# One attention state for the linear-attention layer, a new order of its steps, and identity products on TensorE ahead of the first projection

## What is computed

```python
c_act = jax.nn.silu(c)
for i in range(DEPTH):
    mod = (c_act @ ada_w[i] + ada_b[i])[:, None, :]
    sh1, sc1, g1, sh2, sc2, g2 = jnp.split(mod, 6, axis=-1)
    h = rms_norm(x, norm_mix_g[i]) * (1 + sc1) + sh1
    y = gla_mixer(...) if i % 2 == 0 else moba_mixer(...)
    x = x + g1 * y
    h = rms_norm(x, norm_mlp_g[i]) * (1 + sc2) + sh2
    x = x + g2 * sq_relu_mlp(h, mlp_w1[i], mlp_w2[i])

# gla_mixer, per chunk of 64 tokens, G = cumulated log decay inside the chunk
q_dec = q * exp(G); k_inv = k * exp(-G); k_tail = k * exp(G_last - G)
A = where(causal, q_dec @ k_inv.T, 0)
U = k_tail.T @ v;  S_next = exp(G_last) * S + U
o = A @ v + q_dec @ S
o = rms_norm(o) * silu(r);  y = o @ w_out
```

## Time and profile before

| | |
|---|---|
| median of 3 runs | 641.33 us (641.04 to 641.89) |
| the profiled execution | 641.9 us |
| span in its trace | 640.1 us, so 1.8 us lie around it |
| TensorE busy | 616.4 us of the span |
| TensorE's mean granted clock | 0.991 |
| DMA | 156.4 MB, 244 GB/s over the span; about 385 GB/s from 6 to 36 us |

### The profile page before, as it was taken

One profiled execution on the slowest core, in us unless ns is written; L12 is line 12 of the kernel. 1 busy time (PEld: TensorE's weight loads), 2 busy tenths in 40 slices (PEclk: granted clock), 3 DMA queues, 4 the chain that ended last, 5 costly groups with the idle time before them and its releaser, 6 DMA issues.

```text
span 640.1 us, 9098 instructions
## 1 busy us (share of the span) xinstructions
PE 616.4 (96%) x3393; PEld 515.5 (81%) x3393; DVE 474.3 (74%) x660; ACT 341.3 (53%) x581; POOL 39.3 (6%) x65
## 2 busy tenths in 40 slices
PE   3799999899999999999999999999999999999997
PEld 2477875677889988998977788888789899899985
DVE  3838998889768978979896898766786555455455
ACT  3446632668645345435558687666954443544440
POOL 3030020000000111101100000000000000000000
PEclk9699999999999999999999999999999999999999
DMA  9999499566588998999982655345376555556501
GB/s 333 387 356 392 150 357 380 215 247 248 193 278 319 373 364 315 388 337 333 355 295 108 226 197 194 132 133 171 128 260 227 179 177 181 192 192 197 197 0 66
DMA packets 59085, 156.40 MB, mean 244 GB/s; under 512 B 2835, under 2 KB 3329, under 8 KB 59057
## 3 DMA queue, kind: packets, MB, share of 16 engines
q1 hardware_dynamic: 47136, 112.34, 49.6%
q0 software_dynamic: 11760, 43.64, 19.1%
q10 hardware_dynamic: 160, 0.07, 0.0%
HBM read 154.98 MB, written 1.05 MB: 244 GB/s over the span
## 4 chain that ended last, share of the span: by engine, by line
PE 84%; DVE 10%; issue 2%; ACT 2%; DMA 1%; ACTq 0%; DVEq 0%
PE ps L501 14%; PE ps L503 14%; PE ps L502 14%; PE ps L700 7%; PE ps L699 7%; PE ps L698 7%; PE ps L508 4%; PE ps L510 3%; PE ps L509 3%; DVE w_lo L1435 1%; PE ps L629 1%; DVE spare L1435 1%; DVE ada_acc L1452 1%; PE ps L620 1%; PE ps L844 1%
## 5 line engine op out<-in xcount | busy, mean ns | idle before, releaser
L1051 ACT ACTIVATE w_hi<-w_raw 128x1024 fp32r<-128x1024 f32 x180 | 189.1, 1058 | 204.8 <-PE ps L503 106.9
L1435 DVE TENSOR_TENSOR w_lo<-w_raw,w_hi 128x1024 fp32r<-128x1024 f32 x180 | 218.0, 1222 | 96.5 <-ACT w_hi L1051 96.3
L700 PE MATMUL ps<-a_hi,w_lo 128*128 128x256 f32 x384 | 108.9, 284 | 0.0
L699 PE MATMUL ps<-a_lo,w_hi 128*128 128x256 f32 x384 | 108.9, 283 | 0.0
L698 PE MATMUL ps<-a_hi,w_hi 128*128 128x256 f32 x384 | 108.8, 283 | 0.0
L501 PE MATMUL ps<-w_hi,m_hi 128*128 128x512 f32 x256 | 100.4, 392 | 0.0
L502 PE MATMUL ps<-w_lo,m_hi 128*128 128x512 f32 x256 | 99.9, 390 | 0.0
L503 PE MATMUL ps<-w_hi,m_lo 128*128 128x512 f32 x256 | 99.8, 390 | 0.0
L501 PE MATMUL ps<-w_hi,a_hi 128*128 128x512 f32 x224 | 92.8, 414 | 4.6 <-DVE a_lo L1590 4.6
L503 PE MATMUL ps<-w_hi,a_lo 128*128 128x512 f32 x224 | 88.7, 396 | 0.0
L502 PE MATMUL ps<-w_lo,a_hi 128*128 128x512 f32 x224 | 88.5, 395 | 0.0
(11 more groups left out here) (204 smaller groups left out, 708.2 us busy)
## 6 DMA issues: line engine op xcount, KB each, us to landing
w_raw<-in_mlp_w_dram SPq DMA_DIRECT2D x64, 1024.0 KB, 5.5
ada_raw<-in_ada_w_dram POOLq DMA_DIRECT2D x40, 1024.0 KB, 6.7
w_raw<-in_gla_w_in_dram SPq DMA_DIRECT2D x12, 1024.0 KB, 13.2
w_raw<-in_moba_w_in_dram SPq DMA_DIRECT2D x12, 1024.0 KB, 7.4
ada_raw<-in_ada_w_dram SPq DMA_DIRECT2D x4, 1024.0 KB, 11.9
arena<-in_ada_w_dram SPq DMA_DIRECT2D x4, 1024.0 KB, 14.3
w_raw<-in_gla_w_out_dram SPq DMA_DIRECT2D x4, 1024.0 KB, 8.9
w_raw<-in_moba_w_out_dram SPq DMA_DIRECT2D x4, 1024.0 KB, 4.8
```

Source lines behind the costliest of these rows:

```text
L699: mm(o, w_hi[:, u, w], a_lo[:, a, :], start=False, stop=False)
L700: z = mm(o, w_lo[:, u, w], a_hi[:, a, :], start=False, stop=u == 3 and k == 1)
L1051: A(dst, w_raw[:, c // 2, c % 2], ACT.Copy).then_inc(hi_made, 1)
L1435: V.tensor_tensor(out, w_raw[:, c // 2, c % 2], w.bitcast(F32), ALU.subtract).then_inc(lo_made, 1)
```

## The change

One state per head: instead of three increments and three chained states, one state per head stands for the first 128 tokens (chunks 0 and 1), and the second 128 use it. Scores inside a 128-token tile between its two chunks are made by eight added products (`k_end`), and the mask is widened to match. Other parts:

- Silu of `c` is made from ScalarE's Exp and three operations on VectorE; the Silu table load ahead of the squares is gone.
- TensorE multiplies the identity by itself 7, 3, 2 and 12 times at four places of `first_norm` (`awake`).
- The zeroing of `att` and the two fills of `restart` go from VectorE to GpSimd. `angles` is split, and most of it goes behind `lo_at(3)`.
- VectorE's `ada()` steps go to other places: the third to (2, 1), ahead of `cumulate`, the fourth to (3, 0); three stand in `out_project`.
- `turn_tail`, `scores`, `update` and `masked` go one to three units later.
- ScalarE makes the first two `o_hi` before the last Silu of r; VectorE's first two `o_low` and `gated(1)` come ahead of the last `lo` of block 6.
- `sum_mods` goes from the end of block 6 to after half unit (0, 2) of block 7, and `turn_mods` from after (0, 1) to after (1, 0).

```diff
@@ GpSimd
+            pool.wait_ge(pos_T, 1)
+            nc.gpsimd.memset(restart[:, :, :], 1.0).then_inc(restart_ok, 1)
+            pool.wait_ge(restart_ok, 1)
+            nc.gpsimd.memset(restart[:, :, 0:1], 0.0).then_inc(restart_ok, 1)
             pool.wait_ge(ada_pe, 6)
...
             for s in range(2, 4 * N_PAIRS_ADA):
+                if s == 5:
+                    pool.wait_ge(qd_ok, 1)
+                    nc.gpsimd.memset(att[:, :, :, :], 0.0).then_inc(zero_ok, 1)
                 pool.wait_ge(ada_mac, 2 * (s - 1))
@@ TensorE
+            def awake(n, bank):
+                for _ in range(n):
+                    mm(ps[:, bank, 0:P], eye[:, :], eye[:, :], start=True, stop=True)
...
                 tr(ps[:, 5, 0:N_ROWS], rows[0:N_ROWS, :], eye[0:N_ROWS, 0:N_ROWS]).then_inc(vec_T, 1)
+                awake(7, 7)
                 ada_rows(2, 0, 7)
                 pe.wait_ge(pos_cp, 2)
                 ada_cols(0, 4)
+                awake(3, 6)
                 ada_rows(2, 1, 7)
                 pe.wait_ge(vec_ok, 1)
+                awake(2, 6)
                 ada_cols(1, 5)
+                awake(12, 6)
...
                 def turn_tail():
                     pe.wait_ge(kd_ok, 1)
-                    for tb in range(TB):
-                        for h in range(GH):
-                            z = tr(ps[:, 2 + tb, h * DK:(h + 1) * DK], k_tailT[:, h, tile(tb)], eye[:, :])
+                    for h in range(GH):
+                        z = tr(ps[:, 2, h * DK:(h + 1) * DK], k_sumT[:, h, :], eye[:, :])
...
+                    for tb in range(TB):
+                        for h in range(GH):
+                            z = mm(ps[0:L, tb, h * P + L:(h + 1) * P], k_end[:, h, tb, :],
+                                   q_dec[:, h, tb * P + L:(tb + 1) * P], start=True, stop=True)
                     z.then_inc(att_p, 1)
...
-                    for c in range(NCH - 1):
-                        q = slice(64 * (c % 2), 64 * (c % 2) + 64)
-                        z = mm(ps[:, 2 * (h % 2) + c % 2, (c // 2) * DV:(c // 2 + 1) * DV],
-                               k_tail[q, c // 2, h, :], g_v[q, c // 2, h * DV:(h + 1) * DV], start=True, stop=True)
+                    for h in (2 * pair, 2 * pair + 1):
+                        z = mm(ps[:, 2 + pair, (h % 2) * DV:(h % 2 + 1) * DV], k_sum[:, h, :],
+                               g_v[:, 0, h * DV:(h + 1) * DV], start=True, stop=True)
...
-                            z = mm(o, att[:, tb, h, :], g_v[:, tb, h * DV:(h + 1) * DV], start=True, stop=True)
-                            for c in (2 * tb, 2 * tb + 1):
-                                if c == 0:
-                                    continue
-                                q = slice(64 * (c % 2), 64 * (c % 2) + 64)
-                                z = mm(o[q], q_dec[:, h, c * L:(c + 1) * L], state[c][:, h, :],
-                                       start=False, stop=True, skip_group_check=True)
+                            z = mm(o, att[:, tb, h, :], g_v[:, tb, h * DV:(h + 1) * DV], start=True, stop=tb == 0)
+                            if tb == 1:
+                                z = mm(o, q_dec[:, h, tile(1)], state[:, h, :], start=False, stop=True)
...
-                         {0: turn_k, 1: turn_q, 3: turn_tail},
-                         {0: scores, 2: lambda: update(0), 3: lambda: update(1)},
-                         {0: lambda: update(2), 1: lambda: update(3), 2: lambda: output(0), 3: lambda: output(1)},
+                         {0: turn_k, 1: turn_q},
+                         {0: turn_tail, 1: scores, 3: lambda: update(0)},
+                         {0: lambda: update(1), 2: lambda: output(0), 3: lambda: output(1)},
...
-                    out_project({0: lambda: turn_o(1), 3: lambda: sum_mods(1, 4)},
-                                {(0, 1): lambda: turn_mods(1, 5)})
+                    out_project({0: lambda: turn_o(1)},
+                                {(0, 2): lambda: sum_mods(1, 4), (1, 0): lambda: turn_mods(1, 5)})
@@ ScalarE
+                act.wait_ge(c_T, 1)
+                A(c_act[:, :], ps[:, 4, 0:KC], ACT.Exp, scale=-1.0).then_inc(c_e, 1)
                 for i in range(2):
                     ada_out(i)
...
+                    (4, 2): [lambda: state_in(0)],
+                    (5, 0): [lambda: state_in(1)],
...
-                    (6, 2): [lambda: read_in(0, 5, [silu_r[:, tb, COLS:D] for tb in range(TB)], ACT.Silu)],
+                    (6, 2): [lambda: o_hi(0, 0), lambda: o_hi(0, 1), lambda: read_in(0, 5, [silu_r[:, tb, COLS:D] for tb in range(TB)], ACT.Silu)],
...
-            nc.scalar.preload_act_table_set(SETS_SILU_SIN)
-            act.wait_ge(c_T, 1)
-            A(c_act[:, :], ps[:, 4, 0:KC], ACT.Silu).then_inc(c_ok, 1)
             nc.scalar.preload_act_table_set(SETS_LN_EXP)
@@ VectorE
-                angles()
+                dve.wait_ge(c_e, 1)
+                link(V.tensor_scalar(c_act[:, :], c_act[:, :], 1.0, None, ALU.add))
+                link(V.reciprocal(c_act[:, :], c_act[:, :]))
+                V.tensor_tensor(c_act[:, :], c_act[:, :], ps[:, 4, 0:KC], ALU.mult).then_inc(c_ok, 1)
+                pos_angles()
...
                 for u in range(2, 4):
                     lo_at(u)
+                angles()
...
             def out_project():
                 for u in range(4):
+                    if u < 3:
+                        ada()
                     lo_at(mix_base[0] + 28 + u)
                 mods(1, 5)
...
-                    (2, 1): [logits], (2, 2): [cumulate], (2, 3): [keys], (3, 1): [queries, zero],
-                    (3, 3): [masked], (4, 1): [lambda: states(0)], (4, 2): [lambda: states(1)],
-                    (5, 0): [lambda: states(2)], (5, 1): [lambda: states(3)],
-                    (5, 3): [ada, o_scales, lambda: normed(0)],
+                    (2, 1): [logits, ada], (2, 2): [cumulate], (2, 3): [keys], (3, 1): [queries],
+                    (4, 0): [masked],
+                    (5, 3): [o_scales, lambda: normed(0)],
...
-                adas = [(2, 0), (3, 1), (3, 2), (4, 0), (4, 2), (5, 0), (5, 2), (6, 1)]
+                adas = [(2, 0), (3, 0), (3, 2), (4, 0), (4, 2), (5, 0), (5, 2)]
                 for n in range(2, 7):
                     for u in range(4):
+                        if (n, u) == (6, 3):
+                            o_low(0, range(2))
+                            gated(1)
                         lo_at(mix_base[0] + 4 * n + u)
...
-                o_low(0, range(2))
-                gated(1)
                 for i in range(2):
                     gate(i, 2 + i)
                 o_low(0, range(2, 4))
-                for _ in range(2):
-                    ada()
```

More of the change, by code:

```diff
@@ L811, in scores, with update @@
                         for h in range(GH):
[L812 to L813 removed]
+                            mm(ps[:, tb, h * P:(h + 1) * P], k_inv[:, h, tile(tb)], q_dec[:, h, tile(tb)],
+                               start=True, stop=True)
+                    for tb in range(TB):
+                        for h in range(GH):
+                            z = mm(ps[0:L, tb, h * P + L:(h + 1) * P], k_end[:, h, tb, :],
+                                   q_dec[:, h, tb * P + L:(tb + 1) * P], start=True, stop=True)
                     z.then_inc(att_p, 1)
[L816 to L820 removed]
+                def update(pair):
+                    if pair == 0:
                         pe.wait_ge(kt_ok, 1)
                         pe.wait_ge(in_out, 6)
[L823 removed]
+                    else:
                         pe.wait_ge(in_out, 8)
[L825 to L829 removed]
+                    for h in (2 * pair, 2 * pair + 1):
+                        z = mm(ps[:, 2 + pair, (h % 2) * DV:(h % 2 + 1) * DV], k_sum[:, h, :],
+                               g_v[:, 0, h * DV:(h + 1) * DV], start=True, stop=True)
                     z.then_inc(u_p, 1)
                 def output(pair):
[L835 removed]
+                    if pair == 0:
+                        pe.wait_ge(att_ok, 1)
+                        pe.wait_ge(qs_ok, 1)
+                        pe.wait_ge(st_ok, 1)
+                    else:
+                        pe.wait_ge(st_ok, 2)
                     for tb in range(TB):
@@ L1189, in tail, with state_in @@
                     act.wait_ge(kt_p, 1)
-                    for tb in range(TB):
-                        z = A(k_tail[:, tb], ps[:, 2 + tb, :].rearrange("p (h d) -> p h d", h=GH), ACT.Copy)
-                    z.then_inc(kt_ok, 1)
+                    A(k_sum, ps[:, 2, :].rearrange("p (h d) -> p h d", h=GH), ACT.Copy).then_inc(kt_ok, 1)
+                def state_in(pair):
+                    act.wait_ge(u_p, pair + 1)
+                    A(state[:, 2 * pair:2 * pair + 2], ps[:, 2 + pair, :].rearrange("p (h d) -> p h d", h=2), ACT.Copy
+                      ).then_inc(st_ok, 1)
                 def o_squares(pair):
@@ L1226, in gla @@
                     (2, 3): [lambda: read_in(0, 1, [g_tok[:, 1, tb] for tb in range(TB)]), decays],
```

(11 more changed lines are left out.)

55 lines of the change are left out of this document (23 added, 32 removed).

## The result

The changed kernel takes 645.9 us (median of 14 runs, 642.95 to 649.42) where the kernel before took 641.43 beside it (14 runs, 640.62 to 643.97): a ratio of 1.0065, with a 95% interval of 1.0051 to 1.0078. It is slower by 0.65%, and above the range that the prediction gave. The profiled execution is one of the quickest, 643.24 us, with a span of 641.4 and a mean granted clock of 0.995; the slower ones stand at 0.988 to 0.992.

What follows compares the result with a forecast made beforehand. TensorE, busy 616 of 640 us, was taken as the bound: its work, clock and few waits. Minus 4.2, minus 6.4, plus 4.4, minus 1.8, plus 6.6 gave minus 1.4 us: 640.5 profiled, 639.9 expected, range 635.8 to 643.9.

Steps and rivals of the forecast that it cites:

- The clock in the new waits: Rival: clock falls behind the wait at the norm's transposes, 642.5; with a second wait doing so, 645.1; chance 0.2.
- The rival's price of 2.6 us for a fall: Each new wait followed by half clock adds 2.6 us, the extra time of a unit at half rate.
- the wait of 1.8 us at 125.5: Wait in the stream of the kernel before, followed by clock 1.00; cited against the clock falling in new waits.
- Part 1, minus 4.2: Start: first projection at 23.8 against 25.91, first unit 2.8 us instead of 5.4, less a 0.5 wait; minus 4.2 us.
- TensorE's wait for the second MB: Start: TensorE asks at 27.5 for its next row product's second MB, landed at 28.0; plus 0.5 us.
- Part 2, minus 6.4: TensorE's attention work: cheaper `update` and `output`, fewer transposes, no masked-score wait, eight score products added; minus 6.4 us.
- Part 3, plus 4.4: VectorE between blocks 2 and 3: moved `ada()` steps make TensorE wait 1.7, 2.2 and 0.6; plus 4.4 us.
- Part 4, minus 1.8: Output projection: earlier `o_low` and `o_hi` remove TensorE's wait ahead of it; minus 1.8 us.
- Part 4, plus 6.6: Behind the projection's start: VectorE's late low part and `mods` ahead of `residual` make TensorE wait 2.4 and 4.5; plus 6.6 us.
- in time: Rival: third load landed when VectorE comes, or its waits are less; between blocks 2 and 3 costs 1.9: 637.4; chance 0.25.
- as late as 13.2 us: Rival: third load takes 13.2 us instead of 9.3, adding 3.9 between blocks 2 and 3: 643.8; chance 0.1.
- The identity products hold the clock: Rival said they don't: at the start first unit at half rate, start costs 1.1 instead of giving 4.2, 645.2; chance 0.05.

Runs made afterwards that it cites:

- number one: Changed kernel with `mods` behind both residual steps of the first tile in `out_project`, a low part for the next block behind them too: 642.35 us, ratio 1.0011.
- the order alone: Kernel before with only the new places of the `ada()` steps, `o_hi`, `o_low`, `gated(1)`, `sum_mods` and `turn_mods`: 655.13 us, ratio 1.0213.
- Number two: Changed kernel with the `ada()` at (2, 1), ahead of `cumulate`, taken away and one put at (3, 1), behind `queries`: 643.98 us, ratio 1.0047.
- the start alone: Kernel before with only Silu from Exp, the identity products, the split of `angles` and `restart` on GpSimd: 641.37 us, ratio 1.0008.
- the attention alone: Kernel before with only the one-state attention and its units, start and order as before: 639.19 us, ratio 0.9965.
- both, old order: Kernel before with the changed start and the one-state attention together, without the new order: 638.44 us, ratio 0.9952.
- the early `o_low`: Kernel before with new start and attention, `o_hi`, first `o_low` and `gated(1)` early, `ada()` steps re-placed, `sum_mods`, `turn_mods`, `mods` later: 637.9 us, ratio 0.9947.

## Why the prediction was wrong

**The clock in the new waits** is what put the time out of the range. The forecast let it hold, at 0.4, and gave its fall 0.2: 642.5 for one place, 645.1 for two. The median is 645.9, and filling the waits without touching any dependence takes 3.2 us off it (2.7 by the ratios), back into the range. That this is the clock is shown. What failed in the forecast's own terms is that a new wait was priced at its length alone. In which of the three waits it falls is not the same from run to run (the profile has it at two of them, that of number one at others), and of the slowest runs no trace exists. The rival's price of 2.6 us for a fall does not hold either. At (2, 3) it is nothing, as shown above; at the norm it is 1.1 to 2.3 in the five profiles that have a fall there (10.8 to 11.9 us from the first transposes to the second, 9.6 to 9.7 at the full clock). The forecast argued from the wait of 1.8 us at 125.5 that was followed by 1.00; it was the nearest row, but the new waits are 2.1 to 4.5, and on that side there was no row at all. The Trainium skill ("TensorE: Matmul & The Clock Gate", section "HAM oscillation — how this bites in real kernels") has waits between bursts return the array to half rate at each of them; that rule, cited for the rival, came true here for all seven waits of 3.35 to 4.34 us, and for nine of twelve between 2.0 and 2.9.

**The profiled execution**, 643.24, is also 2.7 above the forecast's 640.5 for it: 0.9 from parts 1 to 3, 0.4 less and 1.0 more from the two halves of part 4, and 1.1 from the half rate behind the norm's transposes. (The other 3.2 of the 6.0 us that the median is off is the place of this execution among its runs, 0.57 above the median in the kernel before and 2.66 below it here.) By its points, against the steps:

- *Part 1, minus 4.2.* The first projection at 23.34 (forecast 23.8) and the clock at 1.00 are right. TensorE's wait for the second MB was put at 0.5 and took 1.57. So 3.5 us were won at the logits. But here stands the other step that failed: the start's gain was carried on as TensorE's own, and alone it is 0.7 us at the second `output` pair and 0 in the time. The DMA transfers, full at some 385 GB/s in the time and profile of before, were read only for the start, and ScalarE's piece at 50 us was not followed.
- *Part 2, minus 6.4.* Its own terms add up to 6.6. Alone it gives 7.4 (the updates are in two pairs of some 0.7, an `output` pair takes 2.4 instead of the 2.6 reckoned); a size off by 1.0, the mechanism right.
- *Part 3, plus 4.4.* The third `ada()` was to wait 2.7 for its MB (from 58.5 to 61.2). In the changed kernel it waited 1.34 (VectorE's order of time):

```profile
58.91 2.61 DVE L1472 SCALAR_TENSOR_TENSOR ada_acc<-ada_raw,c_act,ada_acc 128x1024 f32<-128x1024 f32 x2 [1.34 <-DMA ada_raw<-in_ada_w_dram]
```

  With the order alone it waited 2.90:

```profile
60.67 2.60 DVE L1452 SCALAR_TENSOR_TENSOR ada_acc<-ada_raw,c_act,ada_acc 128x1024 f32<-128x1024 f32 x2 [2.90 <-DMA ada_raw<-in_ada_w_dram]
```

  TensorE's waits at (2, 3) and (3, 0) came where they were put: 2.45 and 0.63 (forecast 1.7 and 2.2). The cost of the part is 3.8 alone (4.6 from the logits), and 2.85 beside the other parts (106.51 against 103.66). Number two shows that a wait of 2.1 at (3, 0) stays when the step is put back; neither the start alone nor the attention alone has one there, so it takes both, TensorE's earlier coming and the longer `keys`.
- Parts 1 to 3 add up to minus 6.2 by the forecast and minus 5.3 by the trace: nearly right by luck, as one term was off by 3.5 one way and two by 1.0 and 1.6 the other way. The sum alone would have hidden that.
- *Part 4, minus 1.8.* The wait ahead of the projection is gone (7.5 us ahead at 119.82; minus 8.0 forecast).
- *Part 4, plus 6.6.* The mechanism is right to the wait: 2.89 at half unit (0, 2) against 2.4, 4.34 at the norm against 4.5. From the projection to the transposes it was 31.16 us, forecast 30.1: VectorE was free at 125.47, 5.65 us into the projection instead of 5.3, and the third `ada()` there waited 1.19 for its load, not 0.55. VectorE's order of time:

```profile
134.04 2.60 DVE L1472 SCALAR_TENSOR_TENSOR ada_acc<-ada_raw,c_act,ada_acc 128x1024 f32<-128x1024 f32 x2 [1.19 <-DMA ada_raw<-in_ada_w_dram]
...
143.93 0.17 DVE L1494 TENSOR_TENSOR modc<-ps,cols 128x16 f32<-128x16 f32 x1 [5.01 <-PE ps L598]
```

VectorE stands 5.01 us at `mods`, with the residual steps behind it in its queue that could have gone ahead. Then half rate behind the transposes adds 1.1 to the second ones (161.74 against 160.52, where the first were only 0.13 late).

**The other rivals.** The third load was neither in time nor as late as 13.2 us. The identity products hold the clock, so that rival fell; but it priced their failure at 5 us, and without them the time is the same.

**What the change's sum hid.** Of the 8.1 us that its two gains bring to the second `output` pair in the old order, 5.2 are left at the projection, where TensorE waits for VectorE, and 3.6 behind the norm. The order that was chosen frees that wait and is 2.3 us ahead of the old one at the projection (119.82 against 122.14), and pays 7.0 us for it behind, so that its span is 4.7 longer (641.4 against 636.7). So most of what is taken from TensorE there is lost as long as VectorE's row of steps between blocks 5 and 7 keeps its length; no kernel here makes that row shorter, so this is argued, not shown.

## What to carry to other kernels

When work is taken from the busiest engine, follow the gain through every later place where another engine or a transfer is nearly as late: a start 3.5 us earlier was worth nothing behind a weight piece that comes at its own time. In an engine's queue, a step that waits for a long way round (sum, copy, turn) goes behind the steps that are ready. Count a new wait of 2 us or more in a dense stream of matmuls with the price of the half clock behind it, unless the next unit waits for another engine in any case, or fill it with products that nobody reads.

## What the runs showed of the hardware

The same wait at the same place is followed by either clock: 2.11 us at (3, 0) by 1.00 in "both, old order" and by 0.50 with the early `o_low` (the two stretches from 72 to 74 us above). Of the waits of 2.0 to 2.9 us in the dense stream behind the first projection that were looked at in these traces, nine were followed by a fall and three were not (2.89, 2.12 and 2.11). Seven waits of 3.35 to 4.34 us all were. The 1.77 ahead of the projection, in the kernel before and with the start alone, was not, nor was the 1.82 of number one, though one of 1.93 at (2, 3) without the identity products was (0.75 in the stretch from 66 to 70 us). So such a wait does not only cost time, it also makes it uncertain: 6.5 us between the changed kernel's runs, 0.7 to 1.6 where the waits are filled. An identity product is 0.23 to 0.25 us at full clock (18 in 4.18, 7 in 1.75 us), a little more than the 0.22 taken from the f32 products.
